# Paged attention in a two-layer decoder: value pages by SyncE's queue, page by page, in place of GpSimd gathers

## What is computed

```python
past_c = pool_ckv[page_table]      # (8, 16, 128, 256): the values, and most of the keys
past_p = pool_kpe[page_table]
s_past = einsum(q_lat, past_c) + einsum(q_pe, past_p)
pr = softmax(concat([s_past * SCALE, s_new], -1))
out = einsum(pr_past, past_c) + einsum(pr_new, ckv)
```

## Time and profile before

| | |
|---|---|
| median of 3 runs | 1531.78 us (1528.43 to 1534.95) |
| the profiled execution's own time | 1531.82 us |
| its span, first to last instruction | 1530.0 us |
| mean granted TensorE clock | 0.989 |
| PE busy | 1479.8 us, 97% |
| DVE, ACT, POOL busy | 67%, 18%, 7% |
| bytes moved | 152.36 MB, of which POOL's queue 16.78 |

### The profile page before, as it was taken

The page is one execution under the profiler, slowest core; times in us unless marked ns, Lnnn a source line. Parts: engine busy times, 40 slices in busy tenths (PEclk is TensorE's granted clock), DMA queues, the critical chain, the costliest instruction groups (busy, mean ns, idle before and its releaser), DMA issues.

```text
span 1530.0 us, 18923 instructions
## 1 busy us (share of the span) xinstructions
PE 1479.8 (97%) x7084; PEld 1189.5 (78%) x7084; DVE 1018.7 (67%) x2068; ACT 269.4 (18%) x564; POOL 103.0 (7%) x114
## 2 busy tenths in 40 slices
PE   7999989899999999999999899999999999999996
PEld 6887735488888888888877778788888888888885
DVE  3363265868776676766865876877866767767845
ACT  4000034412101001001233321121001011011232
POOL 0002223400000000000200001300000000000100
PEclk9999999999999999999999999999999999999998
DMA  8205677712222222222203211222222222222201
GB/s 320 102 33 165 181 212 211 255 56 83 83 83 83 83 84 83 83 83 97 83 28 142 72 67 55 87 83 81 79 82 79 81 80 80 81 81 95 81 28 59
DMA packets 39470, 152.36 MB, mean 100 GB/s; under 512 B 6674, under 2 KB 19379, under 8 KB 26707
## 3 DMA queue, kind: packets, MB, share of 16 engines
q1 hardware_dynamic: 34258, 134.37, 25.4%
q0 software_dynamic: 5120, 16.78, 3.7%
HBM read 148.11 MB, written 3.02 MB: 99 GB/s over the span
## 4 chain that ended last, share of the span: by engine, by line
PE 90%; DVE 5%; DMA 2%; issue 1%; POOL 1%; SPq 0%; ACT 0%; DVEq 0%; POOLq 0%
PE psum L530 69%; PE psum L500 15%; PE psum L658 1%; DMA arena<-in_keys 1%; DMA ring<-in_weights 1%; PE psum L485 1%; DMA arena<-in_rows,vidx 1%; PE psum L764 1%; POOL arena L434 0%; PE psum L729 0%; PE psum L785 0%; PE psum L826 0%; DVE arena L1151 0%; PE psum L693 0%; PE psum L643 0%
## 5 line engine op out<-in xcount | busy, mean ns | idle before, releaser
L530 PE MATMUL psum<-arena 128*128 128x272 f32 x2016 | 478.9, 393 | 0.0
L530 PEld LDWEIGHTS psum<-arena 128*128 128x128 f32 x2016 | 383.0, 190 | 78.6
L1151 DVE TENSOR_TENSOR arena<-psum,arena 128x272 f32<-128x272 f32 x564 | 249.0, 441 | 248.5 <-PE psum L530 226.1
L530 PE MATMUL psum<-B,ring 128*128 128x272 f32 x736 | 184.7, 393 | 3.2 <-issue 1.8
L500 PE MATMUL psum<-A,ring 128*128 128x272 f32 x704 | 169.8, 403 | 9.0 <-DMA ring<-in_weights 7.8
L500 PEld LDWEIGHTS psum<-A,ring 128*128 128x128 f32 x704 | 136.8, 195 | 40.7 <-issue 11.8
L530 PE MATMUL psum<-arena,ring 128*128 128x272 f32 x672 | 167.7, 392 | 0.0
L530 PEld LDWEIGHTS psum<-B,ring 128*128 128x128 f32 x736 | 139.0, 190 | 32.6 <-issue 2.6
L530 PE MATMUL psum<-A,ring 128*128 128x272 f32 x608 | 152.6, 393 | 1.6 <-DVE A L1594 1.5
L530 PEld LDWEIGHTS psum<-arena,ring 128*128 128x128 f32 x672 | 127.4, 190 | 26.0
L530 PEld LDWEIGHTS psum<-A,ring 128*128 128x128 f32 x608 | 115.4, 190 | 26.0 <-DVE A L1594 2.0
(11 more groups left out here) (224 smaller groups left out, 1250.8 us busy)
## 6 DMA issues: line engine op xcount, KB each, us to landing
ring<-in_weights SPq DMA_DIRECT2D x98, 1024.0 KB, 4.8
arena<-in_keys SPq DMA_DIRECT2D x128, 144.0 KB, 2.9
arena<-in_attw SPq DMA_DIRECT2D x1, 3072.0 KB, 20.9
h<-in_xT SPq DMA_DIRECT2D x4, 544.0 KB, 7.8
out_yT<-A SPq DMA_DIRECT2D x8, 272.0 KB, 2.3
arena<-in_pemb SPq DMA_DIRECT2D x2, 544.0 KB, 5.8
ring<-in_weights SPq DMA_DIRECT2D x2, 512.0 KB, 6.8
arena<-in_bias SPq DMA_DIRECT2D x1, 640.0 KB, 8.5
```

Of the source, the lines that this page charges most:

```text
L530: end = pe.matmul(bank(g, n), lhs[:, c, :], x(c), start=c == 0, stop=c == 3)
L1151: ins = dve.tensor_tensor(out, bank(g, n), more, ALU.add)
```

## The change

The tile `vidx`, its load, its two POOL instructions and all gathers are gone; POOL does nothing in the attention any more. SP gets a routine `values(s)`: one register load of 8 page numbers (they stand in `pt` in the order of the key sets), the wait that POOL had, and 8 DMAs, a page each, of 64 partitions by 2 KB: the first four pages to partitions 0 to 63, the other four to 64 to 127. The waits of sets 10 to 13 on `sc_full` are gone. The value sets stand between key sets in SP's one order, and the last eight behind key set 15 and ahead of weight units 9 to 12. TensorE's wait counts 8 DMAs of 16 for a set in place of 4.

```diff
+            rows = a["rows"].rearrange("o (i t) r -> o i (t r)", t=2)
+            def values(s):
+                _, pages = nc.values_load_multi_w_load_instructions(
+                    pt[0:1, 8 * s:8 * s + 8], engines=[sp.engine], min_val=0, max_val=POOL - 1,
+                    skip_runtime_bounds_check_because="the entries of a page table are pages of the pool")
+                if s < 2:
+                    sp.wait_ge(psum_full, T_QL + 1)
+                elif s < 6:
+                    sp.wait_ge(psum_full, T_COL[2 * (s + 3) + 1] + 1)
+                else:
+                    sp.wait_ge(v_used, {6: 1, 7: 2, 8: 7, 9: 8, 14: 9, 15: 10}.get(s, s - 7))
+                for i in range(8):
+                    j, bb = divmod(i, 4)
+                    sp.dma_start(v_buf(v_slot(s))[64 * j:64 * j + 64, bb, :],
+                                 rows[bass.ds(pages[i], 1), :, :].rearrange("o i n -> (o i) n"))\
+                      .then_inc(v_loaded[v_slot(s)], 16)
             for m in range(2):
                 keys(m)
             for u in range(4, 9):
                 unit(u)
-            for m in range(2, 10):
-                keys(m)
+            values(0)
+            values(1)
+            keys(2)
+            values(2)
+            keys(3)
+            keys(4)
+            values(3)
+            keys(5)
+            keys(6)
+            values(4)
+            keys(7)
+            keys(8)
+            values(5)
+            keys(9)
...
-            for m in range(10, 16):
+            values(6)
+            keys(10)
+            values(7)
+            for m in range(11, 16):
                 keys(m)
+            for s in (10, 11, 8, 9, 12, 13, 14, 15):
+                values(s)
...
-            pool.wait_ge(psum_full, T_QL + 1)
-            for s in range(16):
-                if 2 <= s < 6:
-                    pool.wait_ge(psum_full, T_COL[2 * (s + 3) + 1] + 1)
-                elif s >= 6:
-                    pool.wait_ge(v_used, {6: 1, 7: 2, 8: 7, 9: 8, 14: 9, 15: 10}.get(s, s - 7))
-                if 10 <= s < 14:
-                    pool.wait_ge(sc_full, 2 * s - 3)
-                for bb in range(4):
-                    pool.indirect_dma_start(
-                        v_buf(v_slot(s))[:, bb, :], None, rows,
-                        bass.IndirectOffsetOnAxis(ap=vidx[:, 0, 4 * s + bb:4 * s + bb + 1], axis=0))\
-                        .then_inc(v_loaded[v_slot(s)], 16)
...
-                pe.wait_ge(v_loaded[v_slot(s)], 64 * (v_use(s) + 1))
+                pe.wait_ge(v_loaded[v_slot(s)], 128 * (v_use(s) + 1))
```

More of the change, by code:

```diff
@@ L164, in build @@
         pt = sb("pt_ids", [1, NB * NPG], mybir.dt.int32)
-        vidx = sb("vidx", [P, 2, 64], mybir.dt.int32)
         psum = ctx.enter_context(nc.psum_tensor("psum", [P, 8, 512], F))
@@ L259, in build @@
         ids_loaded = sem("ids_loaded")
-        vidx_loaded = sem("vidx_loaded")
         k_loaded = [sem(f"k_loaded{i}") for i in range(4)]
         v_loaded = [sem(f"v_loaded{i}") for i in range(6)]
-        vidx_step = sem("vidx_step")
         consts = sem("consts")
@@ L356, in _ @@
             sp.dma_start(arena[:, 4352:10496], a["attw"]).then_inc(attw_loaded, 16)
-            sp.dma_start(vidx[:], a["vidx"]).then_inc(vidx_loaded, 16)
             sp.dma_start(pt[:], a["page_table"]).then_inc(ids_loaded, 16)
@@ L1752, in lay_out @@
         "page_table": ids.reshape(1, -1),
-        "vidx": np.stack([np.concatenate([np.repeat(ids.reshape(16, 2, 4)[:, j].reshape(1, -1), 64, 0) for j in range(2)], 0),
-                          np.tile(r[:, None] % 64, (1, 64)).astype(np.int32)], 1),
         "keys": np.concatenate([pool, n["cache_kpe"][0]], 2).transpose(0, 2, 1).reshape(POOL, 3, 96, PAGE)
```

## The result

The changed kernel takes 1543.46 us (median of 6 runs, 1541.72 to 1546.19); the kernel before took 1531.12 beside it (6 runs, 1528.43 to 1534.95). The ratio is 1.0085, 95% interval 1.0067 to 1.0102: slower by 12.3 us. The forecast was 1525.1, with a range of 1520.5 to 1532.0. The profiled execution took 1545.88 us.

What follows compares the result with a forecast made beforehand. TensorE, busy 97% of 1530.0 us, was taken as the bound, so only its idle or slow time counted. Terms 4.5 + 2.5 + 0 + 0.3 - 0.6 = 6.7 us off 1531.82 gave 1525.1, range 1520.5 to 1532.0.

Steps and rivals of the forecast that it cites:

- I take 0.50: SP's issue price per value page, taken from key pages: 0.50 us, 4.55 a set; bounds 0.45 to 0.77.
- One for one beyond: Weight unit 9 behind value set 15: lands by 292.3, read at 293.3, nothing lost; delay past 1 us cover costs fully.
- The rule against the change: Value pages on 64 partitions reach 8 of 16 ports: 0.6 us a page, set 11 1.6 later, 5.1 us gain left.
- Rival 3: 64-partition pages drain at half rate, SP's order bounds: at 1.0 us a page, 1549; slower from 0.85; chance 0.08.
- Key sets 10 and 11: Behind value sets on SP: set 10 lands 224.2 (wait 2.1 us), set 11 233.3 (wait 2.9), scored 3.4 earlier.
- rival 2: At key sets 10 and 11: queue as full as before, last pages land in 8.4 us, not 3.2; 1530.0; chance 0.12.
- Rival 1: New wait ahead of key set 11 lets the clock fall, costing the 3.5 us again: 1528.6; chance 0.22.
- ends before the 2.9 us after which the clock was still full: Ahead of key set 10: a 2.1 us wait ends before the clock falls, so 6.2 us to set 11.
- the term 4.5 of the sum: At key set 15: 3.4 us from set 11's earlier score plus the 1.1 us wait that goes.
- Cost 0 for value sets 0 to 5: 27 us of SP's time fits into its 61.3 us of waits for scores; cost zero, 1 us of cover.
- GpSimd's end: Without gathers one DVE form takes 0.29 us, not 0.50; gain 0 to 1 us, 0.3 taken.
- The slow issues: One or two slow issues allowed among the 32 pages leading to key set 11, 0.45 us each: 0.6 us lost.

Runs made afterwards that it cites:

- pages of 128 partitions without the mark: The 128-partition kernel with `nc.dge_precook` set to False for the value loads alone: 1543.14 us, ratio 1.0070 to the kernel before.
- the 128-partition kernel: The changed kernel with each value page as 128 rows of 1 KB on 128 partitions, not 64 of 2 KB on 64: 1531.88 us, ratio 1.0002.
- the kernel with unit 9 ahead: The 128-partition kernel with weight unit 9 issued ahead of value set 15 instead of behind it: 1529.63 us, ratio 0.9982 to the kernel before.
- key sets first: The 128-partition kernel with key sets 10 and 11 issued ahead of value set 6, key set 12 ahead of value set 7: 1534.14 us, ratio 1.0019.

## Why the prediction was wrong, step by step

**The step that failed** is the first term, "I take 0.50": the price of a value page was taken from the key page as "the same instruction". It isn't the same issue. It measured 0.65 us a page and, without a slow issue among the eight, 5.8 us a set, not 4.55. The trace of before had a warning: SP's issues in it have no one price. Weight units 9 to 12 take 327 to 366 ns, but the load of the tile `in_pemb`, also to 128 partitions, takes 433:

```profile
L393 SPq DMA_DIRECT2D arena<-in_pemb x1: 433/433/433, 720.2 to 720.2; - x1
```

The bounds held the measured price (0.45 to 0.77), but they were never carried through the sum. At 0.65 the prediction's own steps put key set 11 at 235.8, the end of key set 15's loads at 251.3, the issue of unit 9 at 298.2 and VectorE's read of it at 304.8 (an estimate: 5.8 us a set, the rest as forecast). That is 7 us later than before, and the gain is a loss. Measured: key set 15's loads ended at 254.4 (248.8 was forecast), the eight value sets took 255.2 to 302.7, the last landed at 304.9, and unit 9 followed at 302.80. "One for one beyond" the 1 us of cover was said of it, and so it went: VectorE's read is 11.0 us later than before, the products 12.6. The 4 us between the estimate and the run are slow issues, 1.5 us of them in the last eight sets, and the later key sets below.

**The rule against the change.** The estimate from it, 0.6 us a page, is near the measured 0.65, but for another reason. It was carried to key set 11 only; carried on to unit 9, the last eight sets alone would have cost 6.4 us against a cover of 1. The Trainium skill, "SBUF — State Buffer", section "Door 1: The DMA port swizzle", has loads of 64 partitions at half the ports. Here pages of 64 partitions at 0.65 us land in 2.7 us and key pages of 96 in 2.5, and pages of 128 partitions without the mark are as slow to issue (475 ns). So this case shows nothing of the rule at this rate; whether it would bound pages that are issued faster no run here shows.

**Rival 3** was the right rival for the end, and its price was wrong. It had the transfer as the cause and let the kernel be slower from 0.85 us a page on. That point left out the register load of each set (with it, 6.8 us a set is 0.78 us a page) and what stood behind value set 15 in the same queue: it counted from the use of the values and not from that of unit 9, whose cover it had just put at 1 us, and it left out the clock. The measured 0.65 costs 12 us. At 0.52 a page, in the 128-partition kernel, the time is that of before (1531.88), not the gain of the forecast.

**Key sets 10 and 11.** Key set 10 was to be in 12.5 us after value set 0's use (224.2 against 211.69) and came 14.2 after it; set 11 21.6 and came 25.7. Sixteen value pages at 0.15 us more are 2.4 us of the 4.1. The landing of the last pages, 2.6 to 3.3 us, was as taken, so rival 2 is out. Rival 1 happened: the clock fell behind both waits, of 3.92 and 2.42 us (0.84 over 208 to 250). Even in the 128-partition kernel, where set 10 waits 3.47, it is 0.53 from 222 to 232. The step "ends before the 2.9 us after which the clock was still full" fails too. In the kernel with unit 9 ahead, a wait of only 2.35 us ended at 222.86, and the clock was at half right behind it:

```profile
222.86:226.50 3.64, 3.64 (x33) 1.97 (x33) 0.00 (x0) 0.00 (x0) 0.00 (x0) 0.53 0.64 183
```

The 6.2 us for the stretch from key set 10 to 11 at full clock was close: it took 5.79 where the clock stayed full (220.75 to 226.54, key sets first).

**The base** was one trace, and its waits aren't fixed. A second trace of the kernel before, on another chip, scores key set 15 at 253.60 in place of 258.63, 5 us earlier, and its products start at 308.00 all the same:

```profile
253.60 1.50 PE L658 MATMUL psum<-arena 96*32 96x256 f32 x24
...
299.01 1.93 PE L693 MATMUL psum<-arena 128*32 128x256 f32 x16 [5.14 <-DMA arena<-in_rows,vidx]
...
308.00 2.10 PE L530 MATMUL psum<-B,ring 128*128 128x272 f32 x8 [0.38 <-DVE B L1550]
```

So in the old kernel an earlier score of key set 15 is taken up by the wait for value set 15, and the term 4.5 of the sum counts only if that wait goes with it. In the 128-partition kernel it went, as said. That key set 15 was scored 3.9 us earlier there (4.5 was said) proves little: the two traces of before differ by more. Cost 0 for value sets 0 to 5 was nearly right: 0.43 us ahead of key set 7. GpSimd's end was worth nothing visible: from the score of set 15 to value set 8 it is 21.8 us before and 21.7 after. The slow issues were under-rated: 7 of 256 page loads took 0.8 to 1.7 us (before: 4 of 128, 0.7 to 1.2), each 0.5 to 1.2 us over the usual on a queue that now sets the pace, where 0.6 was allowed in all.

**What was not foreseen at all** is that the change takes away a cost that depends on the chip. The changed kernel takes 1543.46 us where the kernel before takes 1531, and 1542.07 where that takes 1552. The kernel before takes 1530 to 1531 on some chips and 1549 to 1552 on two.

## What to carry to other kernels

Before moving loads to a queue, ask for each load what its issue costs in the very form in which it will be built, and carry the dear end of that price through the whole line, down to the last thing queued behind it. Look in the trace for other issues on the same queue that take longer. A cover of 1 us is no cover for a line of 64 loads. The best version found here (sets 6 and 7 gathered, the rest on SP in pages of 128 partitions, weight unit 9 ahead of value set 15) takes 1528 to 1529 us on both chips where it ran, not told from the kernel before on the one (0.9984, 0.9963 to 1.0005) and 1.4% under it on the other (0.9860, 0.9839 to 0.9882). A key ring two sets deep leaves hardly any room in its queue: reordering moved the idle from key set 10 to 12 or 13 and won nothing.

## What the runs showed of the hardware

- 1 to 4% of these loads take 0.7 to 2.1 us, in every kernel. The places are not random: in the eight traces with all 256 pages on SP, one of the 91st to 93rd page is slow each time (at 176.6 to 180.3 us), and one of the 208th to 211th (at 261.4 to 270.1). Why is open.
- The TensorE clock fell to its 1.2 GHz level around idles of 2.35 to 5.9 us in this stretch, and stayed there for 3 to 17 us. It did not fall at every such idle: at the 2.48 us ahead of value set 15 in the kernel before it stayed at 1.00.
- In kernels with gathers of GpSimd, VectorE and ScalarE, and at times GpSimd and SP's issues, stopped together for 1 to 6 us on two of five chips; the kernel before was 18 to 21 us longer on these.
